# Three changes joined: scores of the recurrence once per head, the memory pair without its norm, the end of the kernel by two chunks with four output transfers

## What is computed

```python
# first block, layer 0 of 2: recurrence, for 4 heads h of 256 features and 2 directions d
mod = silu(cond) @ ada_w[layer] + ada_b[layer]            # of the input's and of the context's condition
q, k, v, o, z, gates, u, zp = split((x * (1 + scale) + shift) @ w_in)
q, k = silu(dwconv(q)), silu(dwconv(k))
s   = (q_t . k_s) * exp(d_ts - m_t)                       # s <= t forward, s >= t backward
num = sum_s s * v_s + w_inter * (cmat q_t)
den = sum_s s + w_inter * (nvec . q_t)
h   = num / maximum(abs(den), exp(-m_t))                  # the directions are added
...
# second block
mem_n = mem * rsqrt(mean(mem * mem) + 1e-6) * norm_mem_w  # 256 tokens of memory
k = mem_n @ xa_w_k                                        # keys of the attention, used much later
...
a = exp(-8 * gate_r * softplus(-rg_lambda))               # rg_lru
...
h = h + (silu(gate) * val) @ w_down
return h * rsqrt(mean(h * h) + 1e-6) * final_norm_w
```

## Time and profile before

| | |
|---|---|
| median of 3 runs | 3224.58 us (3224.16 to 3226.3) |
| the profiled execution, own time | 3225.4 us |
| its span, first to last instruction | 3223.6 us |
| mean granted TensorE clock | 0.984 |
| busy: PE, DVE, ACT, POOL | 3112.8, 2256.2, 1617.5, 56.6 us |
| loads and stores | 666.43 MB, mean 207 GB/s |

### The profile page before, as it was taken

The page is one execution under the profiler, slowest core; times in us unless marked ns, Lnnn a source line. Parts: engine busy times, 40 slices in busy tenths (PEclk is TensorE's granted clock), DMA queues, the critical chain, the costliest instruction groups (busy, mean ns, idle before and its releaser), DMA issues.

```text
span 3223.6 us, 45072 instructions
## 1 busy us (share of the span) xinstructions
PE 3112.8 (97%) x16882; PEld 2673.6 (83%) x16882; DVE 2256.2 (70%) x2760; ACT 1617.5 (50%) x1940; POOL 56.6 (2%) x52
## 2 busy tenths in 40 slices
PE   6998988999999999999999999999999999999997
PEld 5887776888788887888888888888888888888886
DVE  6878785778858877754767865567557777777554
ACT  5754441455643556544456655445445555555442
POOL 0003300000000000000000000000000000000000
PEclk8999999999999999999999999999999999999998
DMA  7976681877567864655555565566445555555553
GB/s 279 358 265 241 216 310 53 305 288 271 188 201 263 283 218 157 212 183 187 164 196 170 165 197 191 185 212 209 149 137 180 190 190 188 182 190 195 189 189 124
DMA packets 179817, 666.43 MB, mean 207 GB/s; under 512 B 20036, under 2 KB 20420, under 8 KB 178248
## 3 DMA queue, kind: packets, MB, share of 16 engines
q1 hardware_dynamic: 177992, 660.09, 60.1%
q10 hardware_dynamic: 1664, 4.19, 0.3%
HBM read 657.91 MB, written 6.29 MB: 206 GB/s over the span
## 4 chain that ended last, share of the span: by engine, by line
PE 85%; DVE 9%; ACT 2%; DMA 2%; DVEq 1%; issue 1%; ACTq 0%; SPq 0%
PE acc L744 45%; PE acc L748 22%; PE acc L755 3%; PE acc L757 3%; PE acc L756 3%; DVE w_lo L1866 3%; ACT w_hi L1235 1%; DMA mod_raw<-in_w_mod 1%; DVE mod_raw L1877 1%; PE msc L702 1%; PE msc L704 1%; PE msc L855 0%; DMA raw<-in_w_mix_out 0%; PE acc L907 0%; PE msc L1135 0%
## 5 line engine op out<-in xcount | busy, mean ns | idle before, releaser
L1866 DVE TENSOR_TENSOR w_lo<-raw,w_hi 128x1024 fp32r<-128x1024 f32 x1020 | 1241.5, 1227 | 580.6 <-ACT w_hi L1235 571.4
L1235 ACT CAST w_hi<-raw 128x1024 fp32r<-128x1024 f32 x1020 | 1061.2, 1049 | 814.0 <-PE acc L748 590.6
L744 PE MATMUL acc<-a_pair,w_hi 128*128 128x512 f32 x2944 | 931.9, 398 | 4.9 <-DVE a_pair L2765 2.4
L748 PEld LDWEIGHTS acc<-a_pair,w_lo 128*128 128x128 f32 x2944 | 554.5, 188 | 131.0
L748 PE MATMUL acc<-a_pair,w_lo 128*128 128x256 f32 x2944 | 580.2, 278 | 0.0
L744 PE MATMUL acc<-b_pair,w_hi 128*128 128x512 f32 x1792 | 571.8, 401 | 8.2 <-issue 4.3
L744 PEld LDWEIGHTS acc<-a_pair,w_hi 128*128 128x128 f32 x2944 | 451.2, 189 | 7.8 <-DVE a_pair L2765 2.8
L744 PE MATMUL acc<-f_pair,w_hi 128*128 128x512 f32 x1408 | 442.4, 396 | 0.0
L748 PEld LDWEIGHTS acc<-b_pair,w_lo 128*128 128x128 f32 x1792 | 339.4, 189 | 80.3
L748 PE MATMUL acc<-b_pair,w_lo 128*128 128x256 f32 x1792 | 354.7, 279 | 0.0
L748 PEld LDWEIGHTS acc<-f_pair,w_lo 128*128 128x128 f32 x1408 | 264.6, 188 | 62.5
(11 more groups left out here) (351 smaller groups left out, 2798.9 us busy)
## 6 DMA issues: line engine op xcount, KB each, us to landing
raw<-in_w_ffn_up SPq DMA_DIRECT2D x176, 512.0 KB, 4.2
mod_raw<-in_w_mod SPq DMA_DIRECT2D x128, 512.0 KB, 5.1
raw<-in_w_ffn_down SPq DMA_DIRECT2D x88, 512.0 KB, 3.3
ada_raw<-in_w_ada SPq DMA_DIRECT2D x64, 512.0 KB, 5.4
raw<-in_w_xa_k SPq DMA_DIRECT2D x32, 512.0 KB, 6.0
raw<-in_w_k SPq DMA_DIRECT2D x32, 512.0 KB, 4.0
raw<-in_w_v SPq DMA_DIRECT2D x32, 512.0 KB, 5.3
raw<-in_w_even_out SPq DMA_DIRECT2D x32, 512.0 KB, 4.7
```

What stands on the lines that cost most here:

```text
L744: pe.matmul(acc[:, bank(stage, g) + m, :], w_h[:, cols], pair[:, :, kc, :], start=begin, stop=False, skip_group_check=True)
L748: mm = pe.matmul(acc[:, bank(stage, g) + m, 0:T], w_l[:, cols], pair[:, 0, kc, :], start=False, stop=end, skip_group_check=True)
L1235: nc.scalar.copy(w_hi[:, slot], source).then_inc(hi_done, 1)
L1866: vec.tensor_tensor(w_lo[:, slot], source, w_hi[:, slot].bitcast(F32), ALU.subtract).then_inc(lo_done, 1)
```

## The change

Three parts, and steps that move to make room for them.

1. *mem_k.* ADA_FIRST is 6. The pair is made of mem * norm_mem_w without the root: high half on ACT (16 ACTIVATE 128x256), low half on VectorE (16 operations). The squares come at j = 4 to 7 and their sums at j = 6 to 9; the root's reciprocal goes to token_scale, and the keys are multiplied by it after the product (`scale=token_scale`, eight operations; the store waits for them). params is loaded before mem, with a semaphore of its own. The softplus of rg_lambda moves to odd_out at j = 8 to 10, the rows of ctx_v and lat_v to j = 12 of those stages.
2. *Recurrence.* h, d = divmod(r, 2). The scores of a head are formed once, for d = 0, and stay for d = 1. V is multiplied with three blocks of the four, those that the mask leaves. `weighted` of the next step stands behind num. The first scores and the turned rows go into lat_q, at j = 13 and 6.
3. *End.* ffn_down runs by_half: VectorE adds 128x512 to x, ACT squares it, VectorE reduces it, TensorE has eight sums instead of four. ACT forms x * final_norm into y_out as chunks are finished; after the reciprocal four TENSOR_TENSOR 128x1024 remain, and SP issues a transfer of 512 KB behind each.

The core of the diff:

```diff
-ADA_FIRST = 10
+ADA_FIRST = 6
...
-    Stage("mem_k", "w_xa_k", "F", 1, groups=4, ada=(0, ADA_UNITS)),
+    Stage("mem_k", "w_xa_k", "F", 1, groups=4, ada=(0, ADA_UNITS), dve=1),
...
-    Stage("ffn_down", "w_ffn_down", "F", 2, group_units=FC // KU, act=1, dve=2),
+    Stage("ffn_down", "w_ffn_down", "F", 2, group_units=FC // KU, act=4, dve=4),
...
-LAM_AT = 20
+LAM_AT = 8
+CTX_ROWS_AT = 12
...
+ROWS_AT = 6
+SCORES_AT = 13
...
-            sp.wait_ge(dve_step, AFTER["final"]["dve"])
-            nc.sync.dma_start(t["out"], y_out[:]).then_inc(y_stored, 16)
-            sp.wait_ge(y_stored, 16)
+            for q in range(4):
+                sp.wait_ge(dve_step, BEFORE["final"]["dve"] + q + 1)
+                nc.sync.dma_start(t["out"][:, 4 * q:4 * q + 4, :], y_out[:, 4 * q:4 * q + 4, :]).then_inc(y_stored, 16)
+            sp.wait_ge(y_stored, 4 * 16)
...
             def mem_sums(j):
-                q = j - 2
+                q = j - 6
...
-                d, h = divmod(r, 4)
+                h, d = divmod(r, 2)
                 if r >= 2:
 
                     steps.wait(dve=MlstmStep.weighted(r - 2))
...
+                if d == 0:
+                    if h < 2:
+                        pe.wait_ge(act_done, ACT_DONE["lat_q"] - 1)
+                    else:
+                        pe.wait_ge(act_done, ACT_DONE["lat_q"])
+                    for j in range(2):
+                        for kc in range(2):
+                            pe.matmul(msc[:, 1 - h % 2, j * T:(j + 1) * T], kf[:, 2 * h + kc, j * P:(j + 1) * P],
+                                      qf[:, 2 * h + kc, :], start=(j == 0 and kc == 0), stop=(kc == 1),
+                                      skip_group_check=True)
+                steps.done(pe.matmul(msc[:, 2 + d, 0:T], pick[:, h, :], rows[:, 14 + d, :], start=True, stop=True))
...
-                    for j in range(2):
+
+                    seen = [j for j in range(2) if (j <= tt if d == 0 else j >= tt)]
+                    for j in seen:
...
                 if j < 4:
                     q = j
+                    if q == 0:
+                        act.wait_ge(params_in, 16)
                     act.wait_ge(mem_in[q], 16)
+                    for c in range(4 * q, 4 * q + 4):
+                        mm = nc.scalar.activation(b_hi[:, c, :], mem[:, c, :], ACT.Copy, scale=col("norm_mem", c))
+                    steps.done(mm)
...
+                if 1 <= j < 5:
+                    q = j - 1
...
+                    for c in range(4 * q, 4 * q + 4):
+                        mm = vec.scalar_tensor_tensor(b_lo[:, c, :], mem[:, c, :], col("norm_mem", c), b_hi[:, c, :].bitcast(F32),
+                                                      ALU.mult, ALU.subtract)
+                        if c % 2:
+                            mm.then_inc(pair_ready, 1)
...
-            run("mem_k", none(), side=mem_chunks, dest=keys_out)
+            run("mem_k", none(), side=mem_chunks, dest=keys_out, scale=token_scale)
...
+                if r + 1 < 8:
+                    weighted(r + 1)
                 dve.drain()
                 den = num[:, 0:2 * VA].rearrange("p (a b) -> p a b", a=2)[:, :, MLSTM_D]
...
-                if r + 1 < 8:
-                    weighted(r + 1)
                 if r + 2 < 8:
                     masked(r + 2)
...
-            run("ffn_down", residual(1.0))
+
+            def residual_by_half(i, g):
+                first = 8 * i + 2 * g
+                part = flat(x)[:, first * T:(first + 2) * T]
+                half = slice(g % 2 * (2 * T), (g % 2 + 1) * (2 * T))
+                ran(vec.tensor_tensor(part, part, flat(buf_a)[:, half], ALU.add))
...
+            for q in range(4):
+                part = y_out[:, 4 * q:4 * q + 4, :]
+                steps.done(vec.tensor_tensor(part, part, bcast(rstd, 4), ALU.mult))
```

196 lines of the change are left out of this document (111 added, 85 removed).

## The result

| | before | after |
|---|---|---|
| median | 3224.9 us (3224.16 to 3226.3, 4 runs) | 3208.1 us (3203.42 to 3211.73, 4 runs) |
| ratio to before, 95% interval | | 0.9949 (0.9936 to 0.9961) |
| span of the profiled execution | 3223.6 us | 3209.9 us |

The change gains 16.8 us, 0.5%; the forecast was 31.4. Six more runs of the changed kernel in another group gave 3208.57 us and 0.9946 (0.9934 to 0.9958). The profiled execution is the longest of the first four (3211.7 with what lies around it), so its stages are read beside those of a second trace.

What follows compares the result with a forecast made beforehand. TensorE, 97% busy, was taken to bound the kernel, leaving 110.8 us idle and half-clock stretches. Gains of 11 (mem_k), 14 (recurrence) and 6.4 (end), together 31.4, gave 3193 us, range 3185 to 3206.

Steps and rivals of the forecast that it cites:

- First sum at 27.5: In mem_k, TensorE's wait for the first sum of squares, behind ACT's queue, would end near 27.5 us.
- The start's gain of 11: mem_k would end at 188.5 us instead of 199.8, a gain of 11, bounds 5 and 16.
- the 14 us by which the transfers are too slow: In mem_k, weight loads too slow by 8.4 us in all, plus ctx's load; ready units offset some, loss taken as 5.
- the path to 183.4: mem_k's end if TensorE set the pace: 151.4 us of work from 27.5, plus 4.5 for half clock and small waits.
- The sign named for being wrong: At the start, the forecast would be wrong if TensorE idled over 15 us after 30.
- rival A: Transfers rule the start and mem_k still ends at about 199.8, so 3204 us in all; chance 0.12.
- The keys' multiplications hide: In mem_k's epilogues, eight multiplications of 0.69 us stand under a busy TensorE; at most 1.4 at each of four outputs.
- The softplus costs 0, bound 2: In odd_out, about 5 us of VectorE work fits its free time: cost 0, bound 2 if one epilogue is held back.
- The rows at unit 12 cost 0: ctx_rows and lat_rows go to later units under a full TensorE: cost 0, bound 2 if one epilogue is held back.
- The recurrence, 14: Recurrence: first results at 494.2, steps of 5.62 and 4.18, results ending at 530.5; gain 14 us, bounds 9 and 16.
- The end, 6.4: Last sums and output: 3.4 us from shorter operations and 3.0 from a smaller last transfer; gain 6.4, bounds 1 and 8.
- Rival C: At the end, output transfers go one behind the other, 4 x 3.3, gaining 0.6: 3199 us; chance 0.04.

Runs made afterwards that it cites:

- a_late: The changed kernel with the root turned at unit 17 of mem_k instead of 13 and ctx loaded without waiting for the turn: 3209.04 us, ratio 0.9945.
- a_noscale: The changed kernel without the eight multiplications of the memory's keys by the root and the store's wait for them: 3198.17 us, ratio 0.9918.
- p_rec: The kernel before with only the recurrence part of the change, including the moved rows of ctx_v and lat_v: 3207.95 us, ratio 0.9950.
- p_mem: The kernel before with only the mem_k part of the change, including the softplus in odd_out: 3225.36 us, ratio 1.0006.
- p_end: The kernel before with only the end part of the change: 3217.72 us, ratio 0.9979.
- a_nomem: The changed kernel with the mem_k part undone, softplus included, recurrence and end as changed: 3200.89 us, ratio 0.9928.

## Why the prediction was wrong

The forecast was 3193 with a range of 3185 to 3206; 3208.1 is outside. Step by step:

- **First sum at 27.5: right.** TensorE's wait for it ends at 27.63, and the waits for pick and the pair are gone.
- **The start's gain of 11: wrong, it was 0 in mem_k.** The step that failed is the credit against the 14 us by which the transfers are too slow: I took 5 as the loss, so up to eight ready units were to cover 9. They don't. There was a second error, in TensorE's position at 60 us: the path to 183.4 has some 121 us of unit work left there, after had 128. The list of moved steps had the reciprocal in it, but no price for the turn behind it (5.0 of wait), and 4.5 for half clock and small waits was too little (10.22 us of work at 0.50 alone cost 5.1). But a_late shows that this was not what decided: it had the forecast's 121 left at 60 us, and lost 16 behind it instead of 5. That this comes near the 14 without any credit is in part chance, as some of it is the keys' work (next item; mem_k ends 4 earlier without it). The sign named for being wrong, TensorE idle for over 15 us after 30, did not show: its waits there are 5.0, 3.5 and 3.3, 11.8 in all. The queues are 0.94 busy from 60 on before and after, and rival A, which had 0.12, was the case; the 4 us beyond its 3204 lie in the next two items.
- **The keys' multiplications hide: wrong.** The prediction named the path, ACT's store waiting with casts behind it, and let TensorE's lead hide it, with 1.4 at each of four outputs as the worst. ACT's waits there were 8.2 at three outputs and 3.8 at the last, 12.0 in all, since a split stands between VectorE's addition and its multiplication. That made the next w_hi and the next piece of ctx's pair late: 2.1 to 3.7 in ctx_k, and without multiplications and wait the kernel is 10 faster (a_noscale). That is the largest term that the sum put at nothing.
- **The softplus costs 0, bound 2: wrong.** 0.9 to 4.0 in odd_out, 2.2 and 4.0 in the two traces of after. VectorE had 19.6 of 110 us free there, as the row said, but a chain of 20 small operations in a row puts 4.9 us ahead of one w_lo, which was 3.3 early: the ring has four places, VectorE's lead at that unit was little more than one unit of 2.8.
- **The rows at unit 12 cost 0: wrong the other way.** In p_rec ctx_v to lat_v take 3.4 less. TensorE's wait for VectorE ahead of lat_k's states falls from 4.8 to 0.2, a new one of 3.9 for ACT's rows comes in ctx_v; the rest is not split up.
- **The recurrence, 14: right.** 14.4 in p_rec's trace, steps of 5.59 and 4.35 where 5.62 and 4.18 were worked out, and in after 35.3 from first to last result where 36.3 was. With the item above that is about p_rec's 17.
- **The end, 6.4: right,** 7.2 alone. The last sum took 0.70, as the clock was still full, and the transfer lands in 2.9. Rival C fell: four transfers, issued 1.2 apart, take 2.9 each and not one after the other. The fixed cost that the Trainium skill states (DMA: Bandwidth & Descriptors, Anatomy of one DMA) is there for transfers issued by GpSimd, and these are SyncE's; one of 512 KB fits its sum here too, but four of them don't add up, since the queues work on several at once.
- **The sum: the parts were added** as if far apart. p_mem, p_rec and p_end give -23.6 alone and -16.8 together by medians. By the ratios, which have the intervals, it is about 21 against 16 to 17, with 3 to 4 either way on each, so that the parts don't add isn't clear of noise. It would explain 4 to 7 of the 15 us missed at most. The price of part one in company is shown (a_nomem), its mechanism only in part.

## What to carry to other kernels

Free time of an engine in a stretch says nothing about how long the work queued behind an inserted chain will be late: ask for the longest row of operations without a split between them, and compare it with how far ahead the next split really is in the trace, not with the depth of the ring. Where weights stream at nearly the full rate of the queues, as here, removing waits of the multiplying engine turned them into waits for weights; first look whether bytes or the ring's turn can be saved. A term that is "hidden" deserves a check for which other engine waits for it in order, and what stands behind that wait. And a gain in a stage that ends at a restart should be counted up to the end of the next unit, since the half clock can move there.

## What was not expected of the hardware

- GpSimd holds VectorE for nearly its whole operation. A GpSimd TENSOR_TENSOR of 128x1024 took 2.39 to 3.31 us, and the VectorE TENSOR_TENSOR beside it ended 0.55 to 1.09 us after it, 2.0 to 2.1 us late.
- TensorE's clock in the wait of the recurrence: with 14 extra matmuls and 4.78 us of idle time behind them it stood at half when the work came, with 2.42 us at full; the first product took 2.94 and 1.57 us. In the second case lat_o's first unit then ran at a mean of 0.63 and took 4.60 instead of 3.03.
- The same wait of 2.37 to 2.38 us in sgu_u was followed by 16 products in 2.05 us in one trace and in 3.52 in another, with a granted clock of 1.00 and of 0.50 to 0.59.
- The end of mem_k differs by 3.8 us (197.9 to 201.7) between traces with the same instructions up to there, of which 1.55 is the clock behind the turned modulation. Whole runs of the kernel before differ by 2.1 us in the first group of four and by 9.5 in one of eleven.
